# Another order for the opening of a two-block kernel, and the modulation chunk asked for ahead of the weights

## The reference

```python
mod = (silu(c) @ w_ada + b_ada)          # 6 vectors of 2048: sh1, sc1, g1, sh2, sc2, g2
h = x * (1.0 + sc1) + sh1
z = h @ w_in + b_in                      # 2048 x 9216; split into z_u, z_v, z_h, z_g
y_a = spatial_gating(gelu(z_u), gelu(z_v), ...) @ w_branch_a
y_b = hyena(z_h, ..., hy_w1, hy_w2, hy_w3, ...) @ w_branch_b
mix = (gate_a * y_a + gate_b * y_b) @ w_o + b_o
x = layer_norm(ALPHA * x + g1 * mix)
# then the feed-forward part, and the whole second block (convolution, then an HGRN mixer)
```

## Time and profile before

| | |
|---|---|
| median of 3 runs (lowest, highest) | 2670.87 us (2670.01, 2671.71) |
| profiled execution: its own time, its span | 2665.9 us, 2664.0 us |
| PE busy | 2543.0 us, 95% |
| DVE busy | 1994.8 us, 75% |
| ACT busy | 1396.5 us, 52% |
| POOL busy | 817.5 us, 31% |
| mean granted clock of PE | 0.98 of 2.4 GHz |
| read from HBM | 525.52 MB |

### The profile page before, as it was taken

One profiled execution on the slowest core, in us unless ns is written; L12 is line 12 of the kernel. 1 busy time (PEld: TensorE's weight loads), 2 busy tenths in 40 slices (PEclk: granted clock), 3 DMA queues, 4 the chain that ended last, 5 costly groups with the idle time before them and its releaser, 6 DMA issues.

```text
span 2664.0 us, 42756 instructions
## 1 busy us (share of the span) xinstructions
PE 2543.0 (95%) x16588; PEld 2315.2 (87%) x16588; DVE 1994.8 (75%) x2574; ACT 1396.5 (52%) x2181; POOL 817.5 (31%) x764
## 2 busy tenths in 40 slices
PE   5799999999999999999999989999899999999979
PEld 3688888889987888888888889999789999999978
DVE  7789777878878785555555579898668888888855
ACT  1344334444455454445544477676556666676653
POOL 0100001002245420001110348984105555666630
PEclk8899999999999999999999989999999999999989
DMA  9988766887866885555555534444445444444424
GB/s 335 376 288 272 252 216 208 271 277 256 291 207 208 269 275 205 190 176 196 190 194 185 190 100 162 151 148 156 144 161 179 141 150 146 156 152 151 151 98 155
DMA packets 147009, 534.60 MB, mean 201 GB/s; under 512 B 16855, under 2 KB 17016, under 8 KB 146424
## 3 DMA queue, kind: packets, MB, share of 16 engines
q1 hardware_dynamic: 143560, 520.35, 57.6%
q0 software_dynamic: 3248, 11.54, 1.3%
HBM read 525.52 MB, written 6.29 MB: 200 GB/s over the span
## 4 chain that ended last, share of the span: by engine, by line
PE 76%; DVE 10%; issue 6%; ACT 5%; DMA 2%; POOL 1%; SPq 0%; DVEq 0%; POOLq 0%; ACTq 0%
PE ps L596 34%; PE ps L600 23%; PE ps L598 6%; PE ps L599 6%; DVE wl L1046 3%; DVE misc L1067 2%; ACT wh L1776 2%; DMA AF<-in_w_ada 2%; PE ps L983 1%; PE ps L658 1%; PE ps L729 1%; PE ps L741 1%; DVE ps L1525 1%; DVE BF L1675 1%; DVE BF L1665 1%
## 5 line engine op out<-in xcount | busy, mean ns | idle before, releaser
L1046 DVE TENSOR_TENSOR wl<-ring,wh 128x1024 fp32r<-128x1024 f32 x784 | 1040.3, 1339 | 388.1 <-ACT wh L1776 387.5
L600 PE MATMUL ps<-A,wl 128*128 128x256 f32 x4480 | 1263.9, 282 | 0.0
L1776 ACT CAST wh<-ring 128x1024 fp32r<-128x1024 f32 x784 | 814.7, 1044 | 348.3 <-PE ps L600 339.6
L600 PEld LDWEIGHTS ps<-A,wl 128*128 128x128 f32 x4480 | 856.1, 191 | 0.4
L596 PE MATMUL ps<-A,wh 128*128 128x512 f32 x2176 | 772.5, 400 | 31.4 <-DVE wl L1046 19.9
L598 PE MATMUL ps<-A,wh 128*128 128x256 f32 x2304 | 675.0, 293 | 15.5 <-DVE A L1050 9.6
L596 PE MATMUL ps<-B,wh 128*128 128x512 f32 x1792 | 638.6, 401 | 21.0 <-DVE wl L1046 8.2
L599 PE MATMUL ps<-A,wh 128*128 128x256 f32 x2304 | 654.8, 284 | 0.0
L596 PEld LDWEIGHTS ps<-A,wh 128*128 128x128 f32 x2176 | 410.2, 189 | 130.9 <-DVE wl L1046 21.5
L600 PE MATMUL ps<-B,wl 128*128 128x256 f32 x1792 | 503.6, 281 | 0.0
L598 PEld LDWEIGHTS ps<-A,wh 128*128 128x128 f32 x2304 | 444.3, 193 | 18.7 <-issue 10.0
(11 more groups left out here) (250 smaller groups left out, 2176.8 us busy)
## 6 DMA issues: line engine op xcount, KB each, us to landing
ring<-in_w_m SPq DMA_DIRECT2D x256, 512.0 KB, 4.5
ring<-in_hgrn_w_in SPq DMA_DIRECT2D x160, 512.0 KB, 3.7
ring<-in_w_ada SPq DMA_DIRECT2D x146, 512.0 KB, 5.3
ring<-in_w_in SPq DMA_DIRECT2D x144, 512.0 KB, 5.7
ring<-in_conv_w_in SPq DMA_DIRECT2D x96, 512.0 KB, 3.8
AF<-in_w_ada SPq DMA_DIRECT2D x46, 512.0 KB, 8.8
ring<-in_w_ab SPq DMA_DIRECT2D x32, 512.0 KB, 5.3
ring<-in_w_o SPq DMA_DIRECT2D x32, 512.0 KB, 5.5
```

Of the source, the lines that this page charges most:

```text
L600: return e.matmul(dst[:, 0:256], lo, x[:, 0, :], start=False, stop=last)
L1046: e.tensor_tensor(low[:], ring[SLOT[h]][:], hi[:].bitcast(F32), ALU.subtract).then_inc(s.lo, 1)
L1776: e.copy(wh[h % NSPLIT][:], ring[SLOT[h]][:]).then_inc(s.hi, 1)
```

## The change

Seven places are given other numbers, and two pieces of code are moved.

- SP: rows 0 to 1023 of `x` are asked for behind chunks 20 and 24 (were 40 and 42), the first four halves of `w_in` behind chunks 28, 32, 36, 40 (were 46, 48, 50, 52). The first half of `hy_w3` is asked for behind chunk 3; the second half is now issued by POOL, once ACT has done chunk 0.
- DVE: a filter is windowed behind every chunk from the fifth on (was two chunks of three); the five remainders of h and the first three `lo` stand 7 to 11 chunks earlier, two of the biases one and two chunks earlier.
- ACT: the first three `hi` stand behind spectra 1, 3, 5 (were 10, 12, 14), tiles of h begin at spectrum 8 (was 6).
- PE: group 0 is summed behind filter 11 (was 8), group 1 behind spectrum 5 (was 0), group 2 behind all spectra (was 12), group 3 behind k-tile 6 of the first tiles (was 4).
- SP, behind the opening: `weights(h + 7)` stands after the chunks of the same h.

```diff
-            if j == 5:
-                for i in range(2):
-                    e.dma_start(w3[64 * i:64 * i + 64], d["hy_w3"][:, 2048 * i:2048 * i + 2048]).then_inc(s.hw3, 16)
+            if j == 3:
+                e.dma_start(w3[0:64], d["hy_w3"][:, 0:2048]).then_inc(s.hw3, 16)
...
-            if j in (40, 42):
-                rows_in((j - 40) // 2)
-            if j in (46, 48, 50, 52):
-                weights((j - 46) // 2)
+            if j in (20, 24):
+                rows_in((j - 20) // 4)
+            if j in (28, 32, 36, 40):
+                weights((j - 28) // 4)
...
         for h in range(H_M2[0]):
-            weights(h + 7)
             paced = h < H_WO + 16 or h >= H_M1[0]
             if h % 2 and paced:
                 for _ in range(chunks_behind(h // 2 + 1) if h < H_AB else 1):
                     if at < 192:
                         chunk(at)
                         at += 1
+            weights(h + 7)
...
         halves_by_turns(0, pbs, lambda k: wait_lo(w, k, 0), True, False,
-                        lambda k: reduce_chunks(3) if k == 4 else None)
+                        lambda k: reduce_chunks(3) if k == 6 else None)
...
-            if chunks.n >= 5 and chunks.n % 3 != 1 and windows < 16:
+            if chunks.n >= 5 and windows < 16:
...
-            if j in (50, 52, 54, 56, 58):
-                made_low((0, 2, 3, 5, 6)[(j - 50) // 2])
-            if j in (56, 59, 61):
-                lo((56, 59, 61).index(j))
+            if j in (43, 44, 46, 47, 49):
+                made_low((0, 2, 3, 5, 6)[(43, 44, 46, 47, 49).index(j)])
+            if j in (45, 48, 51):
+                lo((j - 45) // 3)
...
+        w.wait_ge(s.sig, 2)
+        e.dma_start(w3[64:128], d["hy_w3"][:, 2048:4096]).then_inc(s.hw4, 16)
```

More of the change, by code:

```diff
@@ L667, in tensor_program @@
             sum_chunk(j)
-        w.wait_ge(s.hw3, 32)
+        w.wait_ge(s.hw3, 16)
+        w.wait_ge(s.hw4, 16)
         for i in range(16):
@@ L675, in tensor_program @@
                      w3[:, n % 4 * 512:n % 4 * 512 + 512], start=True, stop=True).then_inc(s.fmm, 1)
-            if i == 8:
+            if i == 11:
                 reduce_chunks(0)
@@ L688, in tensor_program @@
             done.then_inc(s.spmm, 1)
[L689 removed]
+            if i == 5:
                 reduce_chunks(1)
[L691 to L692 removed]
+        reduce_chunks(2)
         pbs = [bank()[:] for i in range(3)]
         halves_by_turns(0, pbs, lambda k: wait_lo(w, k, 0), True, False,
[L699 removed]
+                        lambda k: reduce_chunks(3) if k == 6 else None)
         for b, k in SECOND:
@@ L1825, in scalar_program @@
             e.copy(ksb[m][:, ri * 512:ri * 512 + 512], ps[3 + i % 3][:]).then_inc(s.spec, 1)
-            if 6 <= i < 14:
-                make_tile(i - 6)
-            if 7 <= i < 15:
-                high(i - 7)
-            if i in (10, 12, 14):
-                hi((i - 10) // 2)
+            if i >= 8:
+                make_tile(i - 8)
+            if i >= 9:
+                high(i - 9)
+            if i in (1, 3, 5):
+                hi(i // 2)
+        high(7)
         hi(3)
```

9 lines of the change are left out of this document (3 added, 6 removed).

## The result

The changed kernel takes 2677.74 us, median of 19 runs (2668.41 to 2685.94), where the kernel before, run beside it on the same chip, has 2670.01 (19 runs, 2662.69 to 2671.84). The ratio is 1.0028 with a 95% interval of 1.002 to 1.0037: slower by 5 to 10 us, where 6.2 us less were forecast. The profiled execution, 2669.6 us with a span of 2667.7, is among the quickest of these runs; it is only 3.7 us over the profiled one of before.

The account below looks back on a forecast made before the run. PE was taken to bound the kernel from 143 us on, and the chain through chunk 63 the opening. Terms -5.5 - 2.7 + 2.0 = -6.2 us gave 2664.7 us from 2670.87; 8-in-10 range 2659 to 2677.

Parts of the forecast that it names:

- Term 3: Loop behind the opening: weights asked for after the chunk make halves later; +2.0 us, ends 0 and +16.
- the chance of a slower kernel: Whole kernel: slower by more than about 0.2%, 5.3 us; chance 0.11, out of 0.17 for halves binding.
- 2T = L + 5.4: `w_in` loop: T is time per tile, L from DVE's chunk end to the half's landing; L 5.8 gives T 5.6.
- nearer to the pairs that have the new order: Two chunk-then-half pairs in the trace, L 5.5 and 6.4; 5.8 taken, against 6.7 from busier-stretch medians.
- The second half of the term: Tiles 24 to 26, two chunks: 9.8 us per tile against about 7.8; two steps lack 4 us, half hidden.
- Term 2: Sum of group 3 on PE: starts at once after chunk 63, but at the low clock; -2.7 us (-4.35 to -1).
- I move it as a block: From the sum's end (bias at 127.03) to the third tile at 142.72: same work, moved earlier unchanged.
- Term 1: Opening: chunk 63 ends at 115.3 instead of 120.8, 3.5 us of waits left; -5.5 us (-8.5 to 0).
- late on the other side: Opening: PE lacks six spectra by chunk 36, DVE waits for group 1's sum; gain shrinks by up to 3.
- The half behind the chunk binds the tiles: Rival, even halves of tiles 4 to 26: late halves eat the gain, +6.4 us or 2677.3; chance 0.17.
- The queue still binds chunk 63: Rival, opening: transfer gaps keep chunk 63 at 120.8; -0.7 us or 2670.2; chance 0.13.
- The sign to look for: Sign of a wrong forecast: PE waiting for `wl` again and again between 200 and 305 us.

Follow-up runs that it names:

- opening_only: Changed kernel with the old order (weights, then chunk) restored behind the opening; 2665.8 us, ratio 0.9989 to the kernel before.
- opening_w3_sp: Changed opening, old order behind it, both halves of `hy_w3` on SP behind chunk 5 as before; 2665.4 us, ratio 0.9990 to the kernel before.
- opening_spread: Changed opening, old order behind; masks, k_dft's second part, identity deferred; spectra stored behind chunks 44, 48, 52, 56, four behind 60; 2667.4 us, ratio 0.9995.
- opening_lag: Changed kernel, chunk still ahead of the weights, but each chunk asked for one block later throughout; 2669.2 us, ratio 0.9998 to the kernel before.

## Why the prediction was wrong, step by step

**Term 3 is the step that failed:** the weights behind the chunk were put at +2.0, with ends at 0 and +16. The order by itself costs some 11 us (8 to 15), inside the ends, and the chance of a slower kernel, 0.11, was too low by far. The mechanism was right: the loop of landing, cast, remainder and chunk binds DVE, 2T = L + 5.4. The size of L was not. I took 5.8, "nearer to the pairs that have the new order", and put aside the 6.7 that the medians of the busy stretch gave. SP asks for chunk, even and odd half within 1.1 us:

```profile
202.62 0.33 SPq L516 DMA_DIRECT2D ring<-in_w_ada  x1
202.99 1.79 SPq L531 DMA_DIRECT2D ring<-in_w_in  x2
208.51 0.33 SPq L516 DMA_DIRECT2D ring<-in_w_ada  x1
```

and in tiles up to half 46 the even half lands 6.5 us after the chunk's issue in the mean of the first profile (17 tiles), 6.7 in the second, with single ones up to 8. By the formula T is 5.95 to 6.05; measured on DVE are 6.02 and 6.14 per tile, against 5.70 before. That is 0.3 to 0.4 us per tile over 16 tiles, 5 to 7 us, of which PE loses 2.6 to 3.7 and the rest is the lead of `lo` over PE. The two pairs came from a stretch where little else was in the queue, and I chose the one value in the range at which the loop is just hidden. (The Trainium skill's fit that the prediction quotes beside it, "DMA: Bandwidth & Descriptors", section "Anatomy of one DMA", is given there for transfers that GpSimd issues; the chunks and weights here are SP's, so its 3.2 us are not a price for them.)

The second half of the term, the tiles with two chunks, had the right size and the wrong cover: of 4 us I took DVE's lead to hide half. By then the tiles with one chunk have spent the lead, nothing is hidden, and 4.2 to 5.2 us are lost in the three executions that have the whole order. About 1.8 of them are a term that the prediction did not have: PE waits 2.3 to 3.3 us for the hyena product and its granted clock falls to 0.50 right behind (5.41 us for 3.62).

**Term 2 half failed.** The sum starts at once and takes 3.57, as forecast (3.4). "I move it as a block" failed: in the first profile 3.85 of 6.27 us at SECOND's start are left at the third tile, in the second 0.65 of 5.03, and in the mean of five executions 2.1. The rows that the prediction read of this block were PE's and DVE's, and in them nothing waits for a load. ACT in the kernel before, and the issues at 127.9 us with the time to landing:

```profile
140.03 1.05 ACT L1776 CAST wh<-ring 128x1024 fp32r<-128x1024 f32 x1 [4.87 <-PE ps L600]
140.99 0.47 ACT L1908 ACTIVATE misc<-ps,vec 128x256 f32<-128x256 f32 x1
...
ring<-in_w_in SPq DMA_DIRECT2D x1, 512.0 KB, 11.4
```

The last row is half 7, asked for at 127.89: it landed at 139.3, and the last spectrum (asked for at 119.9, 20.0 us) at 139.9, in the kernel before, 0.8 and 1.1 us before ACT used them. They stood right behind what was binding. The queue was full there (415 GB/s from 121 to 140 us) and the change takes no byte out of it, so moving PE's work earlier could bring no more than about 1 us and what the queue itself won. The low clock in SECOND, 1.2 us in four of the five executions, was not foreseen either.

**Term 1 was mis-sized:** chunk 63 ends at 117.1 to 118.8, 2.0 to 3.7 us earlier instead of 5.5. The waits for chunks fell to 1.6, better than the 3.5 I left. Against that stand 1.1 to 1.4 us of a later first window, which is the new places of `hy_w3` (put at 0), 0.8 to 2.5 us of waiting for PE at bias 1 (the prediction's own "late on the other side", which came true and makes the difference between the executions), and about 1.3 us of slower DVE instructions in the trace after (the remainders `Al` 0.52 for 0.42 us in the mean, one addition 1.75 for 1.28). The Trainium skill's rule ("DMA: Bandwidth & Descriptors", section "Rules for kernel authors") that two transfers to disjoint halves of the partitions serialize even from two engines fits: the later of the two halves landed at 21.7 us from two queues (opening_only) and at 21.6 from one (opening_w3_sp), and the window's load at 27.9 instead of 26.5. So the second queue brought nothing.

**The rivals.** "The half behind the chunk binds the tiles" is what happened, with its 4 us in the two-chunk tiles near the 4.2 to 5.2 that were lost there, and the point that it named, L over 6.6, is about where L was found (6.5 and 6.7). That its 2677.3 is within 0.5 us of the median is in part luck: it charges the one-chunk tiles 10.6 us where PE lost 2.6 to 3.7, and sets against it a gain of 8.2 in the opening where 2.6 were had. "The queue still binds chunk 63" was wrong at chunk 63 and right one step later. The sign to look for, PE waiting for `wl` again and again, was hardly there in the first profile (1.3 us in three waits); up to half 58 the loss shows on ACT, in its many waits, and in DVE's lead, and on PE mostly in one wait at 303.8 us, for another product of DVE.

## What to carry to other kernels

- In a queue that issues in order, a wait belongs to everything behind it. Before putting an item ahead, ask whether its own condition is met at that moment; asking for the item one block later, with the condition long met, took nearly all the waits away.
- Where a loop's period hangs on a latency, take the latency of the loaded stretch, and its mean with the late ones, not the best pairs; where the outcome turns at a value within the measured spread, as here at 6.6, the forecast should be split there.
- What is made ahead of its use hides a loop that is too slow until it is used up. Follow the offset on the engine that bounds the kernel too: here DVE had lost 7.4 us at half 44 where PE had lost 2.3, and PE paid at the next place where DVE had more to do. A lead can be counted on only once.
- To move a piece of the critical path earlier, list what else arrives just in front of its end, by landing times and not by waits: a load that lands 1 us before its use shows no wait in the profile, and is the new bound after 1 us of gain. And count the bytes that must pass before that point: if the queue is full there, only fewer bytes help. None of the versions that only reordered the loads was clearly quicker than opening_only, which is the one to keep, or opening_w3_sp with `hy_w3` as before; neither is clearly quicker than the kernel before.

## What the runs showed of the hardware that was not expected

Between halves 344 and 440 (1190 to 1453 us) an execution either keeps to the time of before within 0.01 us or takes 5.12 us more; of 20 profiled executions 7 are of the second kind, of kernels of every sort, and the difference is the same 5.12 each time. It grows evenly, by 0.32 us per six halves from the first to the last of them. The granted clock is 1.00 in both. From 1250 to 1300 us, opening_spread (of the first kind) and opening_lag (of the second):

```profile
1250.00:1300.00 50.00, 50.00 (x290) 44.10 (x289) 28.90 (x36) 26.09 (x37) 6.66 (x10) 1.00 0.57 189
```

```profile
1250.00:1300.00 50.00, 50.00 (x285) 43.36 (x284) 28.23 (x35) 25.97 (x36) 6.65 (x9) 1.00 0.55 185
```

PE is busy for all 50 us in both and gets through 2% fewer matmuls (285 for 290). The granted clock doesn't show it, and what it is stays open. It is a good part of the spread of 9 us that the runs of the kernel before have among themselves, and a reason to compare executions by the offset at a place and not by their ends.
